# Attention of a decoder trunk: where TensorE takes its waits within a step

## The chip, the cores and the metric

The kernel runs on one core of a Trainium2 chip. The metric is the device time of one execution in microseconds (us). The engines are named as in the profile: PE is TensorE's matmuls, PEld its weight loads (they overlap the matmuls), DVE is VectorE, ACT is ScalarE, POOL is GpSimd, SP issues most DMAs. Each engine works through its own instructions in order, and engines wait for each other on semaphores.

## What is computed

A trunk of two layers on 1024 tokens of width 1024. Layer 0 mixes tokens by sparse attention with three branches (compressed blocks, selected blocks, a sliding window), layer 1 by attention to the 256 keys that an indexer selects. After each comes a gated convolutional feed-forward part; RMS norms stand around all of them. Cut to the part that the change touches:

```python
s_c = jnp.einsum('bqghd,bngd->bghqn', qb, k_cmp)      # compressed branch, "cmp"
s_s = jnp.einsum('bqghd,bgqkd->bghqk', qb, k_s)       # selected blocks, "full"
s_w = jnp.einsum('bqghd,bkgd->bghqk', qb, k_w)        # window, "near"
p = masked_softmax(s, mask)                           # for each branch
o = jnp.einsum('bghqk,bkgd->bqghd', p, v)
o = gb[..., 0:1] * o_c + gb[..., 1:2] * o_s + gb[..., 2:3] * o_w
```

## The kernel before, in words

The attention of a layer is a list of items, written out in full (no loop on the chip). There are 16 rounds, one for each pair of heads and each half of 512 tokens; in a round each branch takes its blocks of 128 keys in turn. An item is one key block for both heads of the pair, up to 512 queries wide (`cmp` is a single item). Layer 0 (`A0`, tiles `n_...`) has 208 items, layer 1 (`A1`, tiles `m_...`) 96. A planner (`AttentionPlan`) places all other work at the steps of this list by its own estimates of cost.

In step s TensorE does, in this order (`attention_pe`):

- the scores of item s+1 (`scores_pe`): for each of the two heads two products (L913, L915) and up to four small ones that add masks (L919). Each head's scores fill one of three PSUM banks in turn (a "unit", bank `u % 3`). Before each head it waits in `bank_free` until ScalarE's exponentials (L976, semaphore `a_ex`) have read the unit three before. For a `cmp` item there is one unit (L888 to L893).
- the ring (`ring_pe`): products that find the row maxima of a later round (`peak_pe`, L851 and, for `cmp`, L845) and one transpose of these maxima per round ("rows", L870). They share three other PSUM banks, `3 + y % 3`. Before ring entry y TensorE waits until VectorE (L1064/L1066, L1081, L1085, semaphore `a_md`) or, for rows, ScalarE (L999, `a_me`) has read entry y-3. A step has none to 13 entries, mostly one to four. The transpose waits besides for all maxima of its round (`a_md`, `a_mc`).
- the values of item s (`values_pe`, L931 and L937) into bank 6 or 7, after a wait for both exponentials of the item, and for the first item of a branch also for the eviction of the bank (L1008, `a_ov`);
- for some steps a branch's row sums (`divisors_pe`, L946 and L951), for which it waits for a bank and for GpSimd's sums (L992, `a_added`).

ScalarE's exponentials of an item run as soon as its scores are there, one head after the other. ScalarE also evicts a branch's result (L1008) into a tile that VectorE's product (L1120) must have freed, and that product needs the reciprocals of the row sums, which travel from ScalarE (L1014) over three DMAs (`n_R<-n_DR`, `r_save<-n_R`, `n_RB<-r_save`, L1178 to L1192). The queries of a round are loaded by DMA (L826) into one of three slots.

In the program a wait is carried by the instruction that follows it. If that one has more waits than it can carry, the further ones stand in an instruction of TensorE's queue of their own ahead of it.

Of the kernel before, what the change touches and what calls it, by code (L numbers as in the profile page):

```python
# [258 lines left out]
def trunk(nc, A, out):  # L259
    ctx = ExitStack()  # L260
    with ctx:
        def semaphore(name):
            return ctx.enter_context(nc.semaphore(name))
# [139 lines left out]
        def bank(b):  # L403
            return PS[:, b, :]
# [292 lines left out]
        def first_norm_pe(pe):  # L697
            for hf in range(2):
                for dt in range(DT):
# [6 lines left out]
        a_rot, a_t1, a_t2, a_qf, a_qhi, a_qlo, a_ready, a_pk, a_md, a_mc, a_me, a_ex, a_pv, a_ov = (  # L706
            semaphore("a_" + x) for x in ("rot", "t1", "t2", "qf", "qhi", "qlo", "ready", "pk", "md",
                                          "mc", "me", "ex", "pv", "ov"))
# [83 lines left out]
        def query_high(r, h, c0=0, w=HALF):  # L792
            return WH[:, r % 3, h * HALF + c0:h * HALF + c0 + w]

        def query_low(r, h, c0=0, w=HALF):
            return WL[:, r % 3, h * HALF + c0:h * HALF + c0 + w]

        def triangle(a):
            return a.B["MZ"][:, 4 * P:5 * P]

        def mask_tile(a, i, kb, count):
            first = i * (i + 1) // 2 + kb
            return a.B["MASK"][:, first:first + count, :].rearrange("p b n -> p (b n)")
# [34 lines left out]
        def peak_pe(pe, a, y, x):  # L838
            p = a.plan.peaks[x]
            if x == 0 or a.plan.peaks[x - 1].r != p.r:  # L840
                pe.wait_ge(a_slot[p.r % 3], a.queries_in(p.r))
            g = a.group(a.order[p.r][0])
            if p.kind == "cmp":
                for ii in range(4):
                    last = nc.tensor.matmul(PS[:, 3 + y % 3, ii * DH:(ii + 1) * DH],  # L845
                                            query_high(p.r, p.h, ii * P, P),
                                            a.B["KCA"][:, g, DH:2 * DH], start=True, stop=True)
            else:
                k0, w = peak_keys(a, p)
                KA = a.B[a.keys[p.kind][0]]  # L850
                last = nc.tensor.matmul(PS[:, 3 + y % 3, 0:w], query_high(p.r, p.h, p.ii * P, P),  # L851
                                        KA[:, g, k0:k0 + w], start=True, stop=True)
            last.then_inc(a_pk, 1)

        def ring_pe(pe, a, step):

            for y in a.plan.ring_at.get(step, ()):
                if y >= 3:
                    what, x = a.plan.ring[y - 3]
                    if what == "peak":  # L860
                        pe.wait_ge(a_md, a.md0 + x + 1)
                    else:
                        pe.wait_ge(a_me, a.me0 + x + 1)
                what, x = a.plan.ring[y]
                if what == "peak":
                    peak_pe(pe, a, y, x)
                else:
                    pe.wait_ge(a_md, a.md0 + a.plan.total[x])
                    pe.wait_ge(a_mc, a.mc0 + a.plan.extra[x])
                    nc.tensor.transpose(PS[:, 3 + y % 3, 0:P], a.B["NM"][:, x % 2, :],  # L870
                                        IDENT[:, :]).then_inc(a_pk, 1)

        def bank_free(pe, a, u):

            if u >= 3:
                pe.wait_ge(a_ex, a.qk0 + u - 2)

        def scores_pe(pe, a, s):
            n = a.plan.items[s]
            B, g, hf = a.B, a.group(a.order[n.r][0]), a.order[n.r][1]  # L880
            if s == a.plan.opens[n.r]:
                pe.wait_ge(a_slot[n.r % 3], a.rows_in(n.r))
            if n.kind == "cmp":
                u = n.u
                bank_free(pe, a, u)
                for h in range(2):
                    c = DH * (1 - h)
                    nc.tensor.matmul(bank(u % 3), B["KCA"][:, g, c:c + P], query_high(n.r, h),  # L888
                                     start=h == 0, stop=False)
                    nc.tensor.matmul(bank(u % 3), B["KCB"][:, g, c:c + P], query_low(n.r, h),  # L890
                                     start=False, stop=False)
                for ii in range(4):
                    last = nc.tensor.matmul(PS[:, u % 3, ii * P:(ii + 1) * P],  # L893
                                            B["CMPM"][:, 4 * hf + ii, :], B["IDB"][:, :],
                                            start=False, stop=ii == 3)
                last.then_inc(qk, 1)
                return
            KA, KB = (B[x] for x in a.keys[n.kind][0:2])
            keys = slice(n.kb * P, (n.kb + 1) * P)
            masks = []  # L900
            for ii in range(n.c0 // P, (n.c0 + n.w) // P):
                i = 4 * hf + ii
                if "MASK" in B and i >= 2:
                    masks.append((ii, mask_tile(a, i, n.kb, 1)))
                elif i == n.kb:
                    masks.append((ii, triangle(a)))
                elif n.far and i == n.kb + 4:
                    masks.append((ii, B["MZ"][:, 0:P]))
            for h in range(2):
                u = n.u + h  # L910
                bank_free(pe, a, u)
                dst = PS[:, u % 3, 0:n.w]
                nc.tensor.matmul(dst, KA[:, g, keys], query_high(n.r, h, n.c0, n.w),  # L913
                                 start=True, stop=False)
                last = nc.tensor.matmul(dst, KB[:, g, keys], query_low(n.r, h, n.c0, n.w),  # L915
                                        start=False, stop=not masks)
                for x, (ii, mask) in enumerate(masks):
                    o = ii * P - n.c0
                    last = nc.tensor.matmul(PS[:, u % 3, o:o + P], mask, B["IDB"][:, :],  # L919
                                            start=False, stop=x == len(masks) - 1)  # L920
                last.then_inc(qk, 1)

        def values_pe(pe, a, s):
            n = a.plan.items[s]
            B, g = a.B, a.group(a.order[n.r][0])
            b = 6 + n.rb % 2
            if n.first and n.rb >= 2:
                pe.wait_ge(a_ov, a.rb0 + n.rb - 1)
            if n.kind == "cmp":
                pe.wait_ge(a_ex, a.qk0 + n.u + 1)  # L930
                nc.tensor.matmul(bank(b), B["VC"][:, g, :], a.probabilities(n, 0), start=True,  # L931
                                 stop=True).then_inc(a_pv, 1)
                return
            pe.wait_ge(a_ex, a.qk0 + n.u + 2)
            V = B[a.keys[n.kind][2]]
            for h in range(2):
                last = nc.tensor.matmul(PS[64 * h:64 * h + 64, b, n.c0:n.c0 + n.w], V[:, g, n.kb, :],  # L937
                                        a.probabilities(n, h), start=n.first, stop=n.last)
            last.then_inc(a_pv, 1)
# [15 lines left out]
        def attention_pe(pe, a):  # L955
            pe.wait_ge(a_ready, a.ready0 + 5)
            plan = a.plan
            ring_pe(pe, a, -1)
            scores_pe(pe, a, 0)
            for s in range(plan.NI + 2):  # L960
                if s + 1 < plan.NI:
                    scores_pe(pe, a, s + 1)
                ring_pe(pe, a, s)
                if s < plan.NI:
                    values_pe(pe, a, s)
                for rb in plan.divisors_at.get(s, ()):
                    divisors_pe(pe, a, rb)
# [1776 lines left out]
```

## Time and profile before

| | |
|---|---|
| Median of 3 runs | 3386.02 us (3385.41 to 3388.66) |
| The profiled execution | 3384.83 us, its span 3383.0 us |
| Attention of layer 0 | about 296 to 885 us of the span |
| Attention of layer 1 | about 2173 to 2495 us |

A row of a timeline is: start in us, duration in us, engine, line, instruction, output and inputs, shapes, how many were merged into the row, and in brackets how long the engine had been idle before it and what ended the idle time ("issue": nothing that the profile shows). The idle time of PEld is not idle time of TensorE: matmuls may run in it. A row of waits gives who waited for whom, the total in us, how many times, and the longest. A chain of waits lists in order of time what each next piece was released by.
### The profile page before, as it was taken

The page shows a single profiled execution, that of the slowest core. Times are in us where ns is not written, and L with a number is a line of the kernel's source. Part 1 is how long each engine was busy: PE and PEld are TensorE (multiplying, and loading weights), DVE is VectorE, ACT ScalarE, POOL GpSimd, SP SyncE. Part 2 cuts the span into 40 slices and gives each one's busy share as a digit, 9 for nine tenths or more (in the row PEclk, how much of TensorE's full clock was granted, in tenths as well). Part 3 has the DMA queues.
Part 4 walks back from the last instruction along what each step waited for, and adds up shares of the span by engine and source line. Part 5 has one row for each costly group of instructions (what it writes and reads, how often), then busy time and mean ns, then how long its engine had stood idle before and what let it go on. Part 6 is the DMA issues. An engine that isn't in the chain of part 4 may idle for free.

```text
span 3383.0 us, 38562 instructions
## 1 busy us (share of the span) xinstructions
PE 2976.0 (88%) x13504; PEld 2177.6 (64%) x13504; DVE 2117.4 (63%) x3711; ACT 1453.6 (43%) x2519; POOL 701.9 (21%) x683
## 2 busy tenths in 40 slices
PE   7797989999879999999968664379997999999997
PEld 5684544445567888878856553244556788887885
DVE  6544455555366776677676699655436676667656
ACT  4342444444434544444433544333444454444443
POOL 2352454544300000000003035425630000000000
PEclk9787999999989999999989787689998999999999
DMA  5143221121322323333322022322132233333332
GB/s 166 44 110 91 48 45 43 39 52 39 116 69 88 97 90 100 99 93 96 94 87 77 0 56 81 94 63 58 42 104 75 87 94 94 100 94 94 98 110 73
DMA packets 360184, 270.51 MB, mean 80 GB/s; under 512 B 63941, under 2 KB 313863, under 8 KB 359479
## 3 DMA queue, kind: packets, MB, share of 16 engines
q1 hardware_dynamic: 358839, 265.96, 27.2%
q8 instruction: 107, 1.75, 0.2%
q10 hardware_dynamic: 1152, 2.10, 0.2%
q14 instruction: 86, 0.70, 0.1%
HBM read 233.46 MB, written 29.82 MB: 78 GB/s over the span
## 4 chain that ended last, share of the span: by engine, by line
PE 71%; DVE 10%; DMA 5%; issue 5%; ACT 4%; POOL 3%; SPq 2%; POOLq 0%; ACTq 0%; DVEq 0%
PE PS L510 18%; PE PS L512 17%; PE PS L511 17%; PE PS L937 5%; PE PS L913 3%; PE PS L851 3%; PE PS L915 2%; DMA n_RB<-r_save 1%; PE PS L919 1%; PE PS L951 1%; DMA WL<-ql_save 1%; DMA r_save<-n_R 1%; SPq L1999 1%; DVE RT_b L615 1%; DVE m_Z L2372 1%
## 5 line engine op out<-in xcount | busy, mean ns | idle before, releaser
L510 PE MATMUL PS<-HH,WH 128*128 128x512 f32 (+1 forms) x2160 | 860.0, 398 | 132.5 <-POOL WL L483 76.4
L511 PE MATMUL PS<-HL,WH 128*128 128x512 f32 (+1 forms) x2160 | 851.8, 394 | 0.0
L512 PE MATMUL PS<-HH,WL 128*128 128x512 f32 (+1 forms) x2160 | 850.5, 394 | 0.0
L510 PEld LDWEIGHTS PS<-HH,WH 128*128 128x128 f32 x2160 | 416.5, 193 | 228.3 <-issue 100.1
L511 PEld LDWEIGHTS PS<-HL,WH 128*128 128x128 f32 x2160 | 416.1, 193 | 87.5 <-issue 2.3
L512 PEld LDWEIGHTS PS<-HH,WL 128*128 128x128 f32 x2160 | 415.0, 192 | 86.7
L499 DVE TENSOR_TENSOR WL<-WR,WH 128x1024 fp32r<-128x1024 f32 x296 | 361.8, 1222 | 136.6 <-ACT WH L492 132.5
L492 ACT ACTIVATE WH<-WR 128x1024 fp32r<-128x1024 f32 x296 | 314.4, 1062 | 122.7 <-PE PS L512 89.9
L992 POOL TENSOR_TENSOR n_ACC<-n_ACC,n_PX 128x384 f32<-128x384 f32 (+3 forms) x320 | 286.2, 924 | 310.7 <-PE PS L937 187.2
L479 POOL TENSOR_TENSOR TOUCH<-WR 128x1 f32<-128x1 f32 x39 | 10.6, 271 | 1107.7 <-PE PS L512 1051.7
L1085 DVE CUSTOM_DVE_ANT_0 n_JUNK<-PS,n_MZ 128x512 bf16<-128x512 f32 (+2 forms) x320 | 146.1, 487 | 131.4 <-PE PS L851 130.0
L992 POOL TENSOR_TENSOR m_ACC<-m_ACC,m_PX 128x512 f32<-128x512 f32 (+3 forms) x160 | 157.8, 1012 | 172.7 <-PE PS L937 89.2
L976 ACT ACTIVATE n_PX<-PS 128x384 f32<-128x384 f32 (+3 forms) x320 | 134.1, 439 | 122.0 <-PE PS L919 103.5
L1431 DVE TENSOR_TENSOR Y_c<-PS,Y_c 128x512 f32<-128x512 f32 x160 | 107.0, 689 | 87.6 <-PE PS L512 87.2
L1431 DVE TENSOR_TENSOR Y_b<-PS,Y_b 128x512 f32<-128x512 f32 x160 | 107.0, 689 | 85.7 <-PE PS L512 85.3
L510 PE MATMUL PS<-HIDH_b,WH 128*128 128x512 f32 x352 | 141.7, 402 | 6.3 <-issue 3.2
L510 PE MATMUL PS<-HIDH_c,WH 128*128 128x512 f32 x352 | 141.9, 403 | 3.9 <-issue 3.2
L512 PE MATMUL PS<-HIDH_c,WL 128*128 128x512 f32 x352 | 139.3, 396 | 0.0
L512 PE MATMUL PS<-HIDH_b,WL 128*128 128x512 f32 x352 | 139.2, 396 | 0.0
L511 PE MATMUL PS<-HIDL_c,WH 128*128 128x512 f32 x352 | 139.1, 395 | 0.0
L511 PE MATMUL PS<-HIDL_b,WH 128*128 128x512 f32 x352 | 139.1, 395 | 0.0
L1085 DVE CUSTOM_DVE_ANT_0 m_JUNK<-PS,m_MASK 128x512 bf16<-128x512 f32 (+3 forms) x160 | 87.7, 594 | 55.6 <-PE PS L851 55.3
(384 smaller groups left out, 5264.5 us busy)
## 6 DMA issues: line engine op xcount, KB each, us to landing
WR<-in_ffn_w_up SPq DMA_DIRECT2D x176, 512.0 KB, 3.8
WR<-in_ffn_w_down SPq DMA_DIRECT2D x88, 512.0 KB, 3.6
WH<-qh_save SPq DMA_DIRECT2D x64, 256.0 KB
n_RB<-r_save SPq DMA_DIRECT2D x96, 128.0 KB, 3.1
WR<-in_nsa_w_out SPq DMA_DIRECT2D x16, 512.0 KB, 3.9
WL<-ql_save SPq DMA_DIRECT2D x32, 256.0 KB
WR<-in_dsa_w_in SPq DMA_DIRECT2D x16, 512.0 KB, 4.5
WR<-in_dsa_w_out SPq DMA_DIRECT2D x16, 512.0 KB, 4.1
```

The costliest lines, as they stand in the source:

```text
L492: nc.scalar.activation(WH[:, x, :], WR[:, r, :], ACT.Copy).then_inc(w_hi, 1)
L499: nc.vector.tensor_tensor(WL[:, x, :], WR[:, r, :], WH[:, x, :].bitcast(F32), ALU.subtract).then_inc(w_split, 1)
L510: nc.tensor.matmul(dst, wh, xh, start=start, stop=False)
L511: nc.tensor.matmul(dst, wh, xl, start=False, stop=False)
L512: return nc.tensor.matmul(dst, wl, xh, start=False, stop=stop)
L851: last = nc.tensor.matmul(PS[:, 3 + y % 3, 0:w], query_high(p.r, p.h, p.ii * P, P), KA[:, g, k0:k0 + w], start=True, stop=True)
L913: nc.tensor.matmul(dst, KA[:, g, keys], query_high(n.r, h, n.c0, n.w), start=True, stop=False)
L937: last = nc.tensor.matmul(PS[64 * h:64 * h + 64, b, n.c0:n.c0 + n.w], V[:, g, n.kb, :], a.probabilities(n, h), start=n.first, stop=n.last)
L976: nc.scalar.activation(a.probabilities(n, h), PS[:, (n.u + h) % 3, 0:n.w], ACT.Exp).then_inc(a_ex, 1)
L992: nc.gpsimd.tensor_tensor(total, total, a.probabilities(n, h), ALU.add).then_inc(a_added, 1)
L1085: nc.vector.tensor_tensor_reduce(out=B["JUNK"][:, x % 2, 0:w], in0=src, in1=mask, scale=1.0, scalar=-3e38, op0=ALU.add, op1=ALU.max, accum ...
L1431: nc.vector.tensor_tensor(y, bank(4 + x % 3), y, ALU.add).then_inc(f.da, 1)
```

## The change

Three waits of TensorE are placed elsewhere. Nothing else is changed: the same products in the same order, the same buffers, and no other engine's program.

1. Scores: the wait for the second head's bank is taken ahead of the first head's products, in place of the first one's own (it is for the later value of the same semaphore, and so covers it).
2. Ring: the waits for the first up to three entries of a step are all taken ahead of the first of them; a fourth and later entry keeps its wait in its place.
3. Values: their waits are taken ahead of the last ring entry of the step, or in their old place if the step has none.

The waits for a round's queries, for the rows in `scores_pe`, for the transpose and for the row sums stay where they were.

```diff
+        def ring_free(pe, a, y):
+            if y >= 3:
+                what, x = a.plan.ring[y - 3]
+                if what == "peak":
+                    pe.wait_ge(a_md, a.md0 + x + 1)
+                else:
+                    pe.wait_ge(a_me, a.me0 + x + 1)
+
         def ring_pe(pe, a, step):
-            for y in a.plan.ring_at.get(step, ()):
-                if y >= 3:
-                    what, x = a.plan.ring[y - 3]
-                    if what == "peak":
-                        pe.wait_ge(a_md, a.md0 + x + 1)
-                    else:
-                        pe.wait_ge(a_me, a.me0 + x + 1)
+            ys = a.plan.ring_at.get(step, ())
+            for y in ys[0:3]:
+                ring_free(pe, a, y)
+            for n, y in enumerate(ys):
+                if n >= 3:
+                    ring_free(pe, a, y)
                 what, x = a.plan.ring[y]
+                if y == ys[-1] and 0 <= step < a.plan.NI:
+                    values_ready(pe, a, step)
                 if what == "peak":
                     peak_pe(pe, a, y, x)
...
+            if not ys and 0 <= step < a.plan.NI:
+                values_ready(pe, a, step)
...
         def scores_pe(pe, a, s):
...
+            bank_free(pe, a, n.u + 1)
             for h in range(2):
                 u = n.u + h
-                bank_free(pe, a, u)
...
+        def values_ready(pe, a, s):
+            n = a.plan.items[s]
+            if n.first and n.rb >= 2:
+                pe.wait_ge(a_ov, a.rb0 + n.rb - 1)
+            pe.wait_ge(a_ex, a.qk0 + n.u + (1 if n.kind == "cmp" else 2))
+
         def values_pe(pe, a, s):
...
-            if n.first and n.rb >= 2:
-                pe.wait_ge(a_ov, a.rb0 + n.rb - 1)
             if n.kind == "cmp":
-                pe.wait_ge(a_ex, a.qk0 + n.u + 1)
...
-            pe.wait_ge(a_ex, a.qk0 + n.u + 2)
```

## Rows read from the trace of the kernel before

**Rows 1.** The page: span, busy time of the engines, chain by engine.

```profile
span 3383.0 us, 38562 instructions
...
PE 2976.0 (88%) x13504; PEld 2177.6 (64%) x13504; DVE 2117.4 (63%) x3711; ACT 1453.6 (43%) x2519; POOL 701.9 (21%) x683
...
PE 71%; DVE 10%; DMA 5%; issue 5%; ACT 4%; POOL 3%; SPq 2%; POOLq 0%; ACTq 0%; DVEq 0%
...
```

**Rows 2.** Windows of both attentions: stretch, engines' busy time, granted clock, DMA.

```profile
...
474.00:546.00 72.00, 65.72 (x339) 34.98 (x338) 39.91 (x121) 30.01 (x67) 35.85 (x40) 0.98 0.20 46
507.20:510.60 3.40, 3.40 (x10) 1.36 (x11) 1.18 (x5) 0.27 (x1) 0.65 (x1) 0.50 0.06 9
...
2400.00:2495.00 95.00, 92.52 (x566) 46.88 (x563) 40.47 (x114) 45.33 (x91) 64.68 (x62) 1.00 0.17 43
...
```

**Rows 3.** Waits of TensorE's matmuls in layer 0's attention, 296 to 885 us.

```profile
...
PE PS L913 <- ACT n_ACC L976: 13.8, 7, 2.8
PE PS L851 <- DVE n_NM L1085: 13.5, 17, 1.4
PE PS L870 <- DVE n_NM L1066: 10.1, 8, 1.5
PE PS L913 <- ACT n_PX L976: 8.2, 7, 1.2
...
```

**Rows 4.** Timeline of TensorE's weight loads, 449.4 to 452.1 us.

```profile
...
450.39 0.14 PEld L951 LDWEIGHTS PS<-n_ACC,ONES 128*64 128x64 f32 x2 [0.29 <-issue]
...
451.77 0.19 PEld L913 LDWEIGHTS PS<-WH,n_KWA 128*128 128x128 f32 x1 [0.81 <-issue]
...
```

**Rows 5.** Timeline of TensorE's matmuls in the same stretch.

```profile
...
450.82 1.03 PE L951 MATMUL PS<-n_ACC,ONES 128*64 128x512 f32 x4
451.78 0.38 PE L913 MATMUL PS<-WH,n_KWA 128*128 128x256 f32 x1
...
```

**Rows 6.** Timeline of the weight loads across a stall of layer 0.

```profile
...
487.43 0.19 PEld L913 LDWEIGHTS PS<-WH,n_KSA 128*128 128x128 f32 x1 [0.24 <-issue]
...
490.25 0.19 PEld L913 LDWEIGHTS PS<-WH,n_KSA 128*128 128x128 f32 x1 [2.21 <-ACT n_ACC L976]
...
490.59 0.69 PEld L851 LDWEIGHTS PS<-n_KSA,WH 128*128 128x128 f32 x3
...
```

**Rows 7.** Chain of waits that ends this stall.

```profile
...
485.25 3.06 DMA n_RB<-r_save
...
488.33 0.70 DVE n_TMP L1120
...
489.71 0.50 ACT n_ACC L976
...
```

**Rows 8.** Timeline of the weight loads after it, 494.9 to 497 us.

```profile
...
495.02 0.19 PEld L913 LDWEIGHTS PS<-WH,n_KSA 128*128 128x128 f32 x1 [2.09 <-ACT n_PX L976]
...
495.51 0.19 PEld L913 LDWEIGHTS PS<-WH,n_KSA 128*128 128x128 f32 x1 [0.19 <-ACT n_PX L976]
...
```

**Rows 9.** Timeline of the weight loads, 504.9 to 507.6 us.

```profile
...
505.05 0.54 PEld L845 LDWEIGHTS PS<-n_KCA,WH 128*128 128x128 f32 x4
507.11 0.14 PEld L870 LDWEIGHTS PS<-IDENT,n_NM 128*128 128x128 f32 x1 [1.52 <-DVE n_CS L1064]
...
```

**Rows 10.** Timeline of VectorE in the same stretch.

```profile
...
505.34 0.41 DVE L1064 TENSOR_TENSOR n_CS<-PS,n_CMPM 128x256 f32<-128x256 f32 x1
...
506.12 0.41 DVE L1064 TENSOR_TENSOR n_CS<-PS,n_CMPM 128x256 f32<-128x256 f32 x1
...
```

**Rows 11.** Timeline of the weight loads at the end of layer 0's attention.

```profile
...
874.51 0.19 PEld L913 LDWEIGHTS PS<-WH,n_KWA 128*128 128x128 f32 x1 [1.08 <-ACT n_PX L976]
...
```

**Rows 12.** Timeline of the weight loads, layer 1, first half.

```profile
...
2199.05 0.19 PEld L913 LDWEIGHTS PS<-WH,m_KDA 128*128 128x128 f32 x1 [0.17 <-issue]
...
2203.02 0.19 PEld L913 LDWEIGHTS PS<-WH,m_KDA 128*128 128x128 f32 x1 [3.35 <-ACT m_ACC L976]
...
```

**Rows 13.** Chain of waits, layer 1, 2262 to 2272 us.

```profile
...
2263.42 5.44 DMA WL<-ql_save
...
```

## Prediction

> **What bounds the kernel.** The page first: TensorE is busy for 88% of a span of 3383.0 us and carries 71% of the chain that ended last, VectorE 10% [rows 1]. The change touches only the two attentions, some 910 us of it (296 to 885 and 2173 to 2495 us). There the windows show TensorE busy for 65.7 of 72 us in layer 0 and for 92.5 of 95 us in the second half of layer 1, the next engine, VectorE or GpSimd, far behind [rows 2]. So TensorE's order and its stalls set the pace, and every wait put earlier in its queue counts in full unless it is over by then, or unless the time is given back in a later stall. The table of waits tells which are real: in layer 0 the matmuls stood idle 13.8 us for an exponential that starts a branch (7 times), 8.2 us for other exponentials (7), 13.5 us for VectorE's maxima (17), and 10.1 us for the transpose's last maxima (8) [rows 3]. Everything else is released before TensorE comes to it.
>
> **What a wait costs that is already over.** This decides whether fewer places with waits can pay. L951 carries one wait, and its second one stands in an instruction of its own ahead of it. Its weights are nevertheless loaded at 450.39 us, while the products before it run; its own matmul comes at 450.82 us [rows 4, 5]. So a wait that is over neither stops the early weight load nor shows a price, and nor does the extra instruction. I take 0 for each wait taken away and each one joined to another. Bounds: a gain of 0.10 us for each values product (second rival), and for the loss nothing that a row shows; I leave it inside the range. The Trainium skill has the rule ("TensorE: Matmul & The Clock Gate", "Step-by-step: what each phase is for"): weight loads are pulled ahead of running matmuls when row groups don't conflict or the background buffer is free. By it waits that are over don't enter; but it would also have the load of L913 pulled ahead behind L951, where the trace has it only at 451.77 us, with its matmul, so the row decides.
>
> **The parts.** An in-order engine on which waits only move forward gains nothing from them; what is left is to add up where they are not yet over.
>
> *Scores.* The second head's bank is free when the exponential of the item's predecessor, first head, is done. In most steps that is over before the first head's load: no cost. The places where it is not:
>
> - A. Seven stalls of layer 0 [rows 3]. One of them: the first head's load goes at 487.43 us, the second's only at 490.25 us [rows 6]. The first head's work sat in the shadow of a chain of DMA, VectorE's product and the exponential, which ends it whatever TensorE does [rows 7]. Now both heads come after it. From first load to second load is 0.49 us in a pair that runs without other hindrance [rows 8]. 7 x 0.49 = 3.4 us. Behind the stall wait the ring, the values, ScalarE's next exponentials and VectorE's maxima, and the chain goes on through them; nothing gives it back.
> - B. Some 5 us later in six rounds the first head starts at 495.02 us, straight after one exponential, and the second's bank is freed 0.45 us later (its load goes at 495.51 us) [rows 8]. TensorE loses 0.45 us, but here the chain runs beside it through DMAs until about 503 us, and TensorE then stands idle before the transpose: loads of L845 at 505.05, of the transpose only at 507.11 us [rows 9]. What comes out is worked out under the ring.
> - C. Seven places where the bank is free 0.10 us too late (382.79, 453.24 us and on): 0.7 us.
> - D. The end of layer 0: the pair at 872.87 us, whose second load waits until 874.51 us [rows 11], costs a first head of 384 columns, 0.46 us; two more (832.7 and 857.6 us) lie ahead of DMA chains and are taken at half, 0.4 us. Together 0.9 us.
> - E. Layer 1: the pair of 2199.05 us, with its second load at 2203.02 us after 3.35 us idle, and six like it until 2316 us [rows 12]. First heads there are 0.42 to 0.76 us long, 3.7 us together. Two of them (2264.5 and 2283.4 us) are followed by TensorE's wait for a load of queries, 5.44 us long in the first case, and hidden behind that [rows 13]: 2.9 us remain. In the second half of layer 1 none is late.
>
> *Ring.* Entries y+1 and y+2 must be free before y goes. In layer 1 they always are. In layer 0, 17 steps are late, by 7.3 us in all: four by 0.50 us right behind the stalls of A, where TensorE now comes 0.49 us later anyway (0 us); six by 0.28 us about 499 us and its like, where B has made TensorE late already (0 us); five by 0.49 to 0.78 us at the transpose, two by 0.03 us. The five: at 505.05 us the last L845 must now wait for the slot that VectorE's L1064 frees at 505.34 + 0.41 = 505.75 us, about 0.75 us later [rows 9, 10]. This takes up B's 0.45 us. Its four products, 0.61 us long, end about 506.45 us; VectorE took them at 506.12 us [rows 10], so the transpose and all behind it come about 0.35 us later. With B: 6 x 0.35 = 2.1 us.
>
> *Values.* Their exponentials are over at the last ring entry in every step of both layers, mostly by more than 1 us: 0 us. The cover is the ring and the scores between; where a step has no ring the wait stays.
>
> **Sum**: 3.4 + 2.1 + 0.7 + 0.9 + 2.9 = 10.0 us. The profiled execution took 3384.8 us, so 3394.8 us; it lies 1.2 us under the median of the runs, so the forecast is 3396.0 us, 0.3% slower. Without anything given back the local losses are 3.4 + 2.9 + 0.7 + 1.3 + 3.7 + 7.3 = 19.3 us; with A alone certain, 3.4 us. Some 0.2%, 6.8 us, is what can be told from no change.
>
> **The rivals.**
>
> - *Given back.* B, C, D and E lie in stretches with DMA chains; if only A comes through, and a part of E, the loss is 3.4 to 6 us: 3391 us, no difference. For it: 5.44 us waits for queries in layer 1 [rows 13]. Against: layer 0's chain runs through TensorE between the stalls. Chance 0.27.
> - *Faster: the values' weights are loaded early.* Place: the first load of L937 in the steps with a ring, about 250. It no longer carries a wait. If it was the wait, and not the change of tile from 128 to 64 columns, that kept it behind the last maxima product, it can now overlap it. Price: L951's products started 0.43 us apart with loads pulled ahead; L913 behind them comes 0.96 us after 450.82 us, where twice 0.43 would be 0.86 [rows 4, 5], so 0.10 us a time, 25 us: 3396 - 25 = 3371 us. It decides from 0.04 us a time (10 us). Against: L951 with its waits is pulled ahead. No row has a change of tile without a wait, so it stays open. Chance 0.08.
> - *Slower still: the clock.* The granted clock was 0.50 from 507.2 to 510.6 us, right behind an idle TensorE, 0.98 on average around it [rows 2]. Such a stretch costs at most half of its 3.4 us. Of the seven stalls of A only one was followed by it. The change makes their idle time unbroken, half a us longer; if the other six and four of E get one, 10 x 1.7 = 17 us more, 3413 us; with half of them 3405 us. The skill's page on TensorE ("Why this matters for your kernels") likewise says that idle gaps between bursts of matmuls cost the clock; by it this would be the likeliest case, by the one in seven of the trace it isn't. Chance 0.12.
> - The forecast itself: 0.53.
>
> **Numbers.** 3396.0 us. The range goes down to 3387 us, most of "given back", and up to 3406 us, all local losses or half of the clock's; outside are the faster rival and the end of the clock's. Slower by over 0.2%: 0.53 + 0.12 = 0.65, less a little for the forecast's lower edge and more for the rival's upper; 0.64. Within: 0.28. Faster: 0.08.
>
> **What would show it.** The count of late waits of L913 for ScalarE stays, but the first load of such a pair, no longer the second, carries it, at the same time in the stall, with both pairs behind it. The transposes' wait shrinks. The load of L937 still starts behind the last ring product: if it starts before it, the faster rival is right. Spans of the two attentions longer by 7 and 3 us, all other stages as before. A granted clock in layer 0 clearly under 0.98 means the clock. Wrong altogether if the attention is shorter.

## The result, and the profile after

The changed kernel takes 3397.9 us (median of 14 runs), the kernel before 3388.3 us (14 runs beside them): 9.6 us more. The ratio is 1.0026, 95% interval 1.0015 to 1.0037, so 5 to 12.5 us slower. The forecast was 10.0 us more, 3396.0 us. Single executions of either kernel lie 15 us apart and more (3383.8 to 3400.2 before), and the profiled one of the changed kernel, at 3393.5 us, is one of its faster ones. Three executions of 7251 to 11364 us (two of the kernel before, one of the last version below) are left out of the comparisons.

In the changed kernel lines have moved: L925 is L913 of before, L931 is L919, L947 L931, L952 L937, L966 L951, L880 L870, L991 L976, L1079 to L1100 are L1064 to L1085. The page, for [rows 1]:

```profile
span 3391.7 us, 38807 instructions
...
PE 2977.4 (88%) x13504; PEld 2180.6 (64%) x13504; DVE 2115.3 (62%) x3711; ACT 1454.8 (43%) x2519; POOL 702.7 (21%) x683
...
PE 72%; DVE 11%; DMA 5%; issue 5%; ACT 4%; POOL 3%; SPq 2%; POOLq 0%; ACTq 0%; DVEq 0%
```

The same work in the same busy time (2977.4 against 2976.0 us), with a span 8.7 us longer. By stages, with the windows of before first (the first stage is left out) and those of after behind them:

```profile
296.00:885.00 589.00, 537.63 (x2703) 285.49 (x2704) 310.86 (x960) 244.09 (x529) 286.21 (x320) 0.96 0.19 44
885.00:2173.00 1288.00, 1072.16 (x4534) 864.11 (x4534) 911.75 (x1374) 573.47 (x910) 145.63 (x113) 0.92 0.28 85
2173.00:2495.00 322.00, 287.51 (x1598) 148.28 (x1598) 157.06 (x466) 126.30 (x262) 157.76 (x160) 0.92 0.22 53
2495.00:3383.00 888.00, 838.61 (x3632) 680.65 (x3632) 582.06 (x739) 384.87 (x608) 0.00 (x0) 0.97 0.31 95
```

```profile
296.90:885.80 588.90, 532.58 (x2704) 284.34 (x2704) 308.73 (x960) 244.94 (x530) 287.13 (x320) 0.97 0.19 44
885.80:2173.00 1287.20, 1071.36 (x4533) 863.51 (x4533) 911.80 (x1374) 572.68 (x909) 145.67 (x113) 0.91 0.28 85
2173.00:2504.00 331.00, 293.50 (x1599) 151.87 (x1600) 158.29 (x467) 127.85 (x262) 157.72 (x160) 0.90 0.21 51
2504.00:3391.70 887.70, 839.06 (x3632) 681.01 (x3628) 581.06 (x739) 384.46 (x606) 0.00 (x0) 0.97 0.31 95
```

All else is as it was; layer 1's attention takes 331.0 us for 322.0, and layer 0's looks the same, where the forecast had 7 and 3 us more. That is a trap of the single profile: layer 0's granted clock is 0.97 for 0.96, layer 1's 0.90 for 0.92. How much of each layer ran at the low clock differs between executions, also where the code is the same. At a lower clock the same products keep TensorE busy for longer (layer 1: 293.5 us at 0.90, 287.5 at 0.92), so TensorE's idle time, the length of a window less its busy time, tells more than the length: in these rows it goes from 51.4 to 56.3 us in layer 0 and from 34.5 to 37.5 us in layer 1. The comparison below uses idle time, stretches without any low clock, and the medians of runs.

TensorE's waits in layer 0, for [rows 3]:

```profile
PE PS L925 <- ACT n_ACC L991: 18.4, 7, 3.5
...
PE PS L851 <- DVE n_NM L1100: 13.5, 17, 1.4
PE PS L925 <- ACT n_PX L991: 9.4, 9, 1.7
PE PS L880 <- DVE n_NM L1081: 8.5, 8, 1.1
```

The seven waits for a branch's first exponential went from 13.8 to 18.4 us, those for the others from 8.2 (7) to 9.4 (9), VectorE's maxima stayed at 13.5, the transpose's wait fell from 10.1 to 8.5. The stall of [rows 6], and the pair behind it of [rows 8]:

```profile
486.42 0.30 PEld L947 LDWEIGHTS PS<-n_ACC,n_VC 128*128 128x128 f32 x2
489.58 0.19 PEld L925 LDWEIGHTS PS<-WH,n_KSA 128*128 128x128 f32 x1 [2.87 <-ACT n_ACC L991]
...
489.92 0.19 PEld L925 LDWEIGHTS PS<-WH,n_KSA 128*128 128x128 f32 x1
...
490.49 0.44 PEld L851 LDWEIGHTS PS<-n_KSA,WH 128*128 128x128 f32 x3
```

```profile
495.31 0.19 PEld L925 LDWEIGHTS PS<-WH,n_KSA 128*128 128x128 f32 x1 [2.57 <-ACT n_PX L991]
...
495.65 0.19 PEld L925 LDWEIGHTS PS<-WH,n_KSA 128*128 128x128 f32 x1
```

Here is the mechanism in four rows. Before, the first head was loaded at 487.43 us and only the second waited. Now nothing of the pair goes before the end of the stall at 489.58 us, 2.87 us idle for the loader, and both heads and their low parts follow: the first maxima load comes 0.91 us after the end of the stall, where it came 0.34 us after it before (490.59 for 490.25) [rows 6]. That is 0.57 us more for this stall, of which the forecast had 0.49. At 495.31 us the second head's load no longer has a wait of its own and follows after 0.34 us.

### The profile page after: what moved, and what is told of

The parts are those of the page before. It is cut to its first block, busy times and chain, and to the rows that moved or that the text cites. A ratio compares the mean times of both kernels' runs of the same rounds, so it can differ in the third digit from the quotient of the medians.

```text
span 3391.7 us, 38807 instructions
## 1 busy us (share of the span) xinstructions
PE 2977.4 (88%) x13504; PEld 2180.6 (64%) x13504; DVE 2115.3 (62%) x3711; ACT 1454.8 (43%) x2519; POOL 702.7 (21%) x683
## 4 chain that ended last, share of the span: by engine, by line
PE 72%; DVE 11%; DMA 5%; issue 5%; ACT 4%; POOL 3%; SPq 2%; POOLq 0%; ACTq 0%; DVEq 0%
PE PS L510 18%; PE PS L511 17%; PE PS L512 17%; PE PS L952 5%; PE PS L925 4%; PE PS L851 3%; PE PS L927 2%; PE PS L931 1%; PE PS L966 1%; DMA n_RB<-r_save 1%; DMA WL<-ql_save 1%; SPq L2014 1%; DVE m_Z L2387 1%; DVE RT_b L615 1%; PE PS L664 1%
## 5 line engine op out<-in xcount | busy, mean ns | idle before, releaser
L510 PE MATMUL PS<-HH,WH 128*128 128x512 f32 (+1 forms) x2160 | 860.6, 398 | 132.5 <-POOL WL L483 77.8
L510 PEld LDWEIGHTS PS<-HH,WH 128*128 128x128 f32 x2160 | 416.6, 193 | 228.5 <-issue 98.1
L1100 DVE CUSTOM_DVE_ANT_0 n_JUNK<-PS,n_MZ 128x512 bf16<-128x512 f32 (+2 forms) x320 | 146.1, 487 | 139.2 <-PE PS L851 138.2
L991 ACT ACTIVATE n_PX<-PS 128x384 f32<-128x384 f32 (+3 forms) x320 | 134.0, 437 | 120.7 <-PE PS L931 116.4
L510 PE MATMUL PS<-HIDH_b,WH 128*128 128x512 f32 x352 | 142.3, 404 | 6.3 <-issue 3.2
L510 PE MATMUL PS<-HIDH_c,WH 128*128 128x512 f32 x352 | 141.9, 403 | 3.9 <-issue 3.2
L1100 DVE CUSTOM_DVE_ANT_0 m_JUNK<-PS,m_MASK 128x512 bf16<-128x512 f32 (+3 forms) x160 | 87.7, 594 | 61.1 <-PE PS L851 60.7
```

The costliest lines, as they stand in the source:

```text
L510: nc.tensor.matmul(dst, wh, xh, start=start, stop=False)
L991: nc.scalar.activation(a.probabilities(n, h), PS[:, (n.u + h) % 3, 0:n.w], ACT.Exp).then_inc(a_ex, 1)
L1100: nc.vector.tensor_tensor_reduce(out=B["JUNK"][:, x % 2, 0:w], in0=src, in1=mask, scale=1.0, scalar=-3e38, op0=ALU.add, op1=ALU.max, accum ...
```

## The experiments

Each ran beside the kernel before on the same chip. The first eight are the kernel before with one part of the change or a piece of one, or with waits added. The last four move work of ScalarE and VectorE; one of them starts from the changed kernel.

### The three parts alone

**Scores alone** (part 1):

```diff
+            bank_free(pe, a, n.u + 1)
             for h in range(2):
                 u = n.u + h
-                bank_free(pe, a, u)
```

> Part 1 of the change alone: the second head's bank is waited for ahead of the first head's scores; ring and values as before. Theory (waits count only where they are not yet over, and this part has nearly all such places): TensorE's first scores start at the end of each of the seven stalls of layer 0, and the loss of the change is nearly all there: 7 to 10 us over the kernel before, of it 3 us or more in layer 1. Rival 'extra instructions' (the 245 wait instructions that the change adds to TensorE's queue cost about 40 ns each): this part adds none, so 0 us. Rival 'ring' (the loss is in the gathered maxima waits): 0 to 2 us.

Measured: 3395.5 us against 3385.9, ratio 1.0027 (1.0017 to 1.0037), 9.6 us slower (5.8 to 12.5). By the medians this is the whole loss.

**Ring alone** (part 2, `ring_free` for `ys[0:3]` ahead of the loop):

> Part 2 alone: the waits of a step's first three ring entries ahead of the first. Theory: without part 1 nothing has made TensorE late, so its own late places show: 0.50 us at four stalls, and little at the transposes, 2 to 4 us in layer 0, 0 in layer 1. Rival 'extra instructions': 161 added wait instructions at 40 ns, 6 us, spread evenly over both layers. Rival 'ring': 8 us or more.

Measured: 3386.3 us, ratio 1.0002 (0.9990 to 1.0014): no difference. The 2 to 4 us expected in layer 0 don't show; the interval reaches to 4.7 us, so they aren't excluded either, and its one clean stretch of layer 0 (below) is a long one.

**Values alone** (part 3, `values_ready` ahead of the last ring entry):

> Part 3 alone: the values' waits ahead of the last ring entry. Theory: 0 us; the exponentials are over by then, and the first weight load behind the last maxima product starts as late as before (320 to 370 ns after the start of a 512 column product), since the change of tile holds it, not the wait. Rival 'early load': 10 to 25 us faster. Rival 'extra instructions': 186 of them at 40 ns, 7 us slower.

Measured: 3387.4 us, ratio 1.0004 (0.9992 to 1.0016): no difference, and 10 us faster is excluded. Whether the load can start early is seen in the changed kernel, at a place of the same shapes in both. The weight loads before, where L937 carries a wait that is long over, and after, where L952 carries none:

```profile
452.48 0.20 PEld L851 LDWEIGHTS PS<-n_KSA,WH 128*128 128x128 f32 x1
452.87 0.20 PEld L937 LDWEIGHTS PS<-n_PX,n_VW 128*64 128x64 f32 x4 [0.19 <-issue]
```

```profile
451.91 0.20 PEld L851 LDWEIGHTS PS<-n_KSA,WH 128*128 128x128 f32 x1
452.30 0.20 PEld L952 LDWEIGHTS PS<-n_PX,n_VW 128*64 128x64 f32 x4 [0.19 <-issue]
```

Both start 0.39 us after the load of the maxima product. It is the same at the other places of layer 0 at full clock: behind a maxima product of 512 columns the first values load starts 0.37 us (median) after the start of that product in the kernel before (60 places), in this one (60) and in the changed one (63). So it isn't the wait that holds the load back. What is left is the change of tile, from 128 to 64 columns; no run varies that alone.

### Waits that are over

```diff
                 bank_free(pe, a, u)
+                pe.wait_ge(proj, a.q0 + 2 * PAIRS)
+                pe.wait_ge(a_ready, a.ready0 + 5)
...
+                    pe.wait_ge(a_ready, a.ready0 + 5)
                 what, x = a.plan.ring[y]
...
             pe.wait_ge(a_ex, a.qk0 + n.u + 2)
+            pe.wait_ge(a_ready, a.ready0 + 5)
```

> The kernel before with waits added that are always over, two ahead of each head's scores and one ahead of each ring entry and each values product; 1424 more wait instructions in TensorE's queue than before. Theory: a wait that is over costs nothing, 0 to 3 us, unless so many in a row keep the queue from running ahead. Rival 'extra instructions': 1424 x 40 ns = 57 us slower.

Measured: 3388.9 us against 3385.9, ratio 1.0005 (0.9994 to 1.0016). At the upper end 5.4 us for 1424 wait instructions, under 4 ns each. At that price the 245 that the change adds are worth less than 1 us; the rival of extra instructions is out.

### Layer by layer

The condition `a.n == 0` or `a.n == 1` around part 1, so that it holds in one layer:

> Part 1 in layer 0 only. Theory by the profiles so far: layer 0's attention gets 4 to 5 us longer for the same low-clock time (the seven stalls at 0.49 us and the chains behind them), layer 1's stays at 322 to 326 us; total 4 to 5 us slower. Rival 'clock': layer 0 not longer once low-clock time is taken off at half, total 0 to 2 us.

> Part 1 in layer 1 only. Rival 'clock': TensorE's idle stretches in layer 1's first half are no longer broken by a first head's scores, some 10 us more of it run at the low clock, and layer 1's attention takes 331 us against 322 to 326; total 5 to 7 us slower, and nothing left once low-clock time is taken off at half. My forecast's term (local losses only): 3 us, with low-clock time as before.

Measured: layer 0 alone 3393.5 us against 3386.9, ratio 1.0019 (1.0008 to 1.0031), 6.7 us; layer 1 alone 3389.8 us, ratio 1.0011 (0.9998 to 1.0023), 3.0 us (-0.7 to 7.8), which taken alone is not clear of none. The forecast had 3.4 + 2.1 + 0.7 + 0.9 = 7.1 us and 2.9 us. My later expectation, that layer 1 would lose 5 to 7 us by the clock, was read off one profile; the median doesn't bear it out, and the interval doesn't exclude it.

What the clock does in layer 1 stays partly open. Three stretches of it, before and with part 1 in layer 1 (two of its irregular first half, one of its second):

```profile
2231.13:2279.12 47.99, 38.54 (x195) 19.66 (x193) 29.90 (x75) 16.79 (x39) 16.20 (x19) 0.86 0.29 67
2279.12:2324.08 44.96, 39.11 (x209) 19.59 (x207) 19.79 (x67) 15.62 (x34) 16.59 (x19) 0.92 0.30 72
2357.69:2395.30 37.61, 37.00 (x220) 18.85 (x218) 20.02 (x63) 16.64 (x31) 22.20 (x22) 1.00 0.23 55
```

```profile
2229.54:2280.85 51.31, 40.47 (x194) 20.97 (x192) 29.95 (x75) 17.20 (x39) 16.36 (x19) 0.80 0.25 63
2280.85:2327.44 46.59, 40.45 (x208) 20.74 (x206) 19.87 (x67) 16.11 (x34) 16.42 (x19) 0.89 0.28 69
2361.06:2398.68 37.62, 37.02 (x220) 18.86 (x218) 20.05 (x63) 16.66 (x31) 22.25 (x22) 1.00 0.22 55
```

The second half is the same to 0.01 us, as forecast. The first half is longer by 3.3 and 1.6 us, at a granted clock of 0.80 and 0.89 for 0.86 and 0.92; 1.9 and 1.3 us of that is TensorE's busy time for the same products. But an unchanged layer 1 can have that as well; this is its whole attention in the run below in which only layer 0 was edited:

```profile
2167.10:2499.50 332.40, 298.53 (x1600) 153.85 (x1600) 156.50 (x467) 127.09 (x262) 157.11 (x160) 0.88 0.22 51
```

332.4 us at 0.88, longer than the changed kernel's 331.0. Over the seven profiles with an unchanged layer 1 it took 322 to 332 us, over the three with part 1 in it 330 to 333. TensorE's idle time parts them better. Taken from the attention's first product to the next stage's first load, it is 32.9 to 36.2 us in the seven (mean 34.6) and 37.3 to 38.2 us in the three (mean 37.7), so 3.1 us more, close to the forecast's 2.9. Whether part 1 also brings more low clock here stays open: those windows have 0.88 to 0.92 in the seven and 0.89 to 0.90 in the three.

### The seven stalls against the other places of layer 0

Part 1 only at the second item of each round of layer 0 (the diff), or only elsewhere in layer 0 (the condition turned round behind `a.n == 0`):

```diff
+            if a.n == 0 and s and a.plan.items[s - 1].first and n.kind == 'full':
+                bank_free(pe, a, n.u + 1)
             for h in range(2):
                 u = n.u + h
-                bank_free(pe, a, u)
+                if not (a.n == 0 and s and a.plan.items[s - 1].first and n.kind == 'full'):
+                    bank_free(pe, a, u)
```

> Part 1 only at the 16 places in layer 0 where a round's second item starts, which holds the seven stalls (term A), and nowhere else. Between the starts of two rounds 71 us apart, in stretches with no low clock, the kernel before takes 70.1 to 70.6 us and part 1 everywhere in layer 0 71.3 to 71.4. By the forecast's terms A is 0.49 us of that: 70.6 to 71.1 us here, 3 to 4 us slower in all. Rival 'A is nothing, the rest is all': 70.1 to 70.6 us. Rival 'all is A': 71.3 us.

> Part 1 in layer 0 everywhere but at those 16 places (terms B, C and D). By the forecast's terms the transposes' chain and the places 0.10 us late give 0.35 + 0.10 us in a clean stretch of 71 us, so 70.5 to 71.0 us, and about 1 us at the end of layer 0: 3 to 4 us slower in all. Rival 'B is given back in the transposes' wait': 70.1 to 70.6 us, only the end longer, 1 us in all. Rival 'they only count together': here and in the other run nothing.

Measured in time: 3393.0 us against 3388.6, ratio 1.0019 (1.0007 to 1.0032), and 3392.6 us, ratio 1.0011 (0.9995 to 1.0027): 4.5 and 4.0 us, the second not clear of none (-1.7 to 9.1), and too near for the times to part them. The clean stretches do it better. Each runs from the first scores of a round to those of the round two further on, at a granted clock of 1.00. In this order: before, the changed kernel, stall places only, other places only.

```profile
607.76:678.30 70.54, 64.33 (x340) 34.54 (x338) 38.90 (x123) 30.27 (x67) 35.86 (x40) 1.00 0.21 47
```

```profile
607.26:678.33 71.07, 64.23 (x341) 34.43 (x339) 38.66 (x123) 30.28 (x67) 35.83 (x40) 1.00 0.20 46
```

```profile
606.77:677.92 71.15, 64.27 (x340) 34.48 (x339) 38.96 (x123) 30.25 (x67) 35.89 (x40) 1.00 0.20 46
```

```profile
462.25:532.90 70.65, 64.38 (x340) 34.61 (x339) 38.96 (x123) 30.14 (x67) 35.84 (x40) 1.00 0.21 47
```

Ten profiles have 28 such stretches. Ten in kernels without parts 1 and 2 in layer 0 take 70.10 to 71.71 us, median 70.5. Nine with part 1 in all of layer 0: 71.03 to 71.55, median 71.1. Stall places only: 70.52, 71.08, 71.15. Other places only: 70.61, 70.64, 70.65, 70.72 and 71.97. The ring alone has a single one, 71.27. So part 1 costs about 0.65 us in 71. By the medians the stall places alone give 0.6 and the others alone 0.2, but with three and five stretches, which spread by 0.6 and 1.4 us, these two are rough.

There are six such stretches in layer 0, with six of the seven stalls: 3.9 us. The last two rounds, with the seventh stall and the places of term D, are longer. They run from their first scores to the first load of the next stage (L510); of the kernels so far five are clean there. The changed kernel's row and the ring alone's:

```profile
821.76:887.17 65.41, 58.69 (x301) 29.13 (x300) 22.28 (x54) 35.28 (x73) 36.82 (x40) 1.00 0.18 46
```

```profile
823.77:887.03 63.26, 58.72 (x301) 29.26 (x299) 23.37 (x54) 35.16 (x73) 37.74 (x40) 1.00 0.19 47
```

The other clean ones are 65.35 us (scores alone), 65.03 (other places only) and 63.34 (values alone): 2.1 us more with all of part 1, 1.7 with the other places only. Together that is 6.0 us, beside 6.7 by the times. Idle time says the same. From the first product of the attention to L510's first load TensorE idles 48.1 to 51.9 us in the five profiles without part 1 in layer 0 (mean 50.2) and 54.9 to 57.4 in the three with it (mean 56.4), 6.2 us more; 53.3 with the stall places only, 54.0 with the others only.

### What the stalls are, and a version that is faster

ScalarE stands in the eviction of a branch (L1008) until VectorE's product has read the tile, with the next exponential queued behind it. The eviction one step later:

```diff
-                if s < plan.NI and plan.items[s].last:
-                    evict_act(act, a, plan.items[s].rb)
+                if 1 <= s <= plan.NI and plan.items[s - 1].last:
+                    evict_act(act, a, plan.items[s - 1].rb)
```

> The kernel before, with ScalarE's eviction of a branch (L1008) one step later, behind the next item's exponentials. It tests what the stalls of A are: if ScalarE waits in the eviction for VectorE's product and holds the next exponential up behind it, the seven waits of L913 for the exponential of n_ACC (13.8 us) shrink to under 5 us, and the kernel gets 5 to 12 us faster. If the DMA chain sets the end of the round anyway, the wait only moves (to the bank of the values, a_ov) and the time stays within 2 us.

> The changed kernel with the same later eviction. If the loss of part 1 in layer 0 is its late places behind ScalarE's stalled eviction, most of it is gone with them: at most 1 to 2 us slower in layer 0 than e7, in layer 1 as much as in e6 unless its stalls go too. If the loss is something else, it stays at 4 to 5 us over e7 in layer 0.

Measured: 3390.4 us against 3386.9 for the first, ratio 1.0012 (0.9996 to 1.0027), no gain; 3391.1 us, ratio 1.0009 (0.9997 to 1.0021) for the change with it. With the stall of ScalarE gone, the change costs 0.7 us by the medians instead of 9.6. That fits the theory but doesn't show it: with both intervals anything up to some 7 us is possible. And the wait only moved, not to the bank of the values, as the expectation's second case had it, but to VectorE. TensorE's waits in layer 0 of the first of the two, then VectorE beside such a place:

```profile
PE PS L851 <- DVE n_NM L1085: 23.7, 32, 1.9
...
PE PS L870 <- DVE n_NM L1066: 12.2, 8, 2.7
...
PE PS L913 <- ACT n_PX L976: 2.1, 6, 0.5
```

```profile
491.38 0.69 DVE L1120 TENSOR_TENSOR n_TMP<-n_OP,n_RB 128x512 f32<-128x512 f32 x1 [2.51 <-DMA n_RB<-r_save]
...
492.72 0.55 DVE L1085 CUSTOM_DVE_ANT_0 n_JUNK<-PS,n_MZ 128x384 bf16<-128x384 f32 x1
```

The waits for exponentials fell from 22.0 to 2.1 us, those for maxima rose from 13.5 to 23.7: VectorE now stands idle for 2.51 us ahead of the product that needs the DMA chain, with the maxima queued behind it. So that product too has to go later in its engine's program:

```diff
-            self.apply_at.setdefault(self.step(t + 11.5), []).append(rb)
+            self.apply_at.setdefault(self.step(t + 13.5), []).append(rb)
-                self.low_at.setdefault(self.step(t + 13.5), []).append(rb // self.nb)
+                self.low_at.setdefault(self.step(t + 15.5), []).append(rb // self.nb)
```

The eviction moves as above, by one step (`items[s - 1]`) or by two (`items[s - 2]`).

> The kernel before with ScalarE's eviction one step later, as in the earlier run, and VectorE's product that waits for the DMA chain (L1120) about 2 us later in its program, behind more maxima. In the earlier run the stall had only gone over to VectorE, which stood 2.5 us ahead of that product with maxima queued behind. If that was all, the waits of L913 for the exponential and of L851 for VectorE's maxima (13.8 and 12.8 us in layer 0 before) both fall, together to under 12 us, and the kernel gets 5 to 12 us faster. If the freed bank or tile is then late instead, they stay at 20 us or more and the time within 3 us.

> The same with the eviction two steps later: should ScalarE in the run with one step again stand in the eviction because the product comes later, this one is freer. Expected 0 to 4 us faster than that run; if the values' first product of a branch then waits for its bank, up to 5 us slower than it, with waits of L937 for L1008 in the table.

Measured: 3379.6 us against 3388.6, ratio 0.9977 (0.9965 to 0.9989), with the eviction one step later; 3377.3 us, ratio 0.9968 (0.9956 to 0.9980), with two: 11 us faster than the kernel before and 20 us under the changed one. The waits of layer 0 in the latter, and both attentions' windows:

```profile
PE PS L870 <- DVE n_NM L1066: 10.7, 8, 1.5
PE PS L851 <- DVE n_NM L1085: 8.5, 16, 1.8
...
PE PS L937 <- ACT n_OP L1008: 1.7, 2, 1.4
PE PS L913 <- ACT n_PX L976: 1.5, 1, 1.5
```

```profile
297.40:860.30 562.90, 534.26 (x2704) 287.68 (x2704) 319.11 (x960) 244.16 (x529) 284.36 (x320) 0.96 0.20 45
2146.50:2488.40 341.90, 301.86 (x1598) 154.69 (x1600) 157.75 (x466) 125.69 (x261) 156.62 (x160) 0.87 0.21 49
```

Waits for exponentials and maxima together came from 35.5 to 10.0 us, and layer 0's attention from 589 to 563 us. Layer 1, whose second half had no such stall, takes 342 us for 322, at a granted clock of 0.87 for 0.92; an unchanged layer 1 reached 332, so the price is some 10 to 20 us and its cause wasn't looked into. The edit in layer 0 alone is the obvious next version; it was not run.

## Why the prediction was right

- **What bounds.** TensorE's own order did, and its late waits were the ones named. Stages outside the attentions kept their times.
- **Waits that are over cost nothing.** Shown directly, at under 4 ns each. With it stands the step built on it, that waits which only move forward gain an in-order engine nothing: no part gained. The Trainium skill's rule ("TensorE: Matmul & The Clock Gate", "Step-by-step: what each phase is for"), by which the load is pulled ahead when row groups don't conflict or the load goes to the background weight buffer, fits the load of L951 at 450.39 us [rows 4]. The first values load behind a maxima product, at 0.37 us with a wait or without, doesn't follow from it as it stands.
- **Term A**, 3.4 us: 0.49 us for each of seven stalls. The clean stretches give 0.6, the stall shown above 0.57. It is half or more of what layer 0 loses. The 0.49 us was right in size by luck: it was read from the pair of 495.02 us [rows 8], whose second load itself waited 0.19 us for an exponential and which term B counts as hindered. An unhindered pair, as at 495.31 us in the changed kernel, has 0.34 us from load to load; the cost is the first head's two products of 512 columns ahead of the second's.
- **Terms B and C and the ring**, 2.8 us: 0.45 us in a stretch by the forecast, 0.2 measured in six, about 1.3 us in all, as far as five stretches tell. This term was sized too large. It said that the last L845 is held until VectorE frees its slot and that the transpose then comes 0.35 us late. In the changed kernel nothing holds it at that place: its load follows the mask's at once, and the transpose's row and VectorE's are

```profile
505.30 0.54 PEld L845 LDWEIGHTS PS<-n_KCA,WH 128*128 128x128 f32 x4
506.99 0.14 PEld L880 LDWEIGHTS PS<-IDENT,n_NM 128*128 128x128 f32 x1 [1.15 <-DVE n_CS L1079]
```

```profile
505.99 0.42 DVE L1079 TENSOR_TENSOR n_CS<-PS,n_CMPM 128x256 f32<-128x256 f32 x1 [1.16 <-PE PS L845]
```

VectorE had come to rest and waited 1.16 us for TensorE; before it had still been busy with older maxima when L845 was loaded [rows 9, 10]. From that load to the transpose's it is 1.69 us now and was 2.06. This one pair doesn't make it the work of the change: the kernel before has both lengths itself, 2.05 to 2.08 us at four of its six such places and 1.68 at two. One of these:

```profile
721.11 0.54 PEld L845 LDWEIGHTS PS<-n_KCA,WH 128*128 128x128 f32 x4
722.79 0.14 PEld L870 LDWEIGHTS PS<-IDENT,n_NM 128*128 128x128 f32 x1 [1.15 <-DVE n_CS L1064]
```

It goes by when VectorE is done with the product that waits for the DMA chain (L1120), which ended 0.24 us ahead of the load of L845 in the kernel before (503.16 + 1.65 = 504.81 us) and 1.87 us ahead of it in the changed one (502.48 + 0.95 = 503.43 us). Over the four profiles with an unchanged layer 0 in which the ring waits are unchanged too (before, values alone, extra waits, scores in layer 1) the short length comes at 12 of 24 places, over the three with part 1 in all of layer 0 at 16 of 18. So TensorE's delay is taken back in the transpose's wait where VectorE was still behind, and that is at about half the places; the forecast had it taken back only in part, and VectorE behind at all six. The hold on L845 does exist: at the first place of this kind, at 362 us, its load waits 0.46 us in the changed kernel, and with the ring alone it waits about 0.5 us at three of seven places.
- **Term D**, 0.9 us: 1.7 measured, in the last two rounds with the other places only. This term was sized too small. It took two of its three places at half because DMA chains follow them; that discount shows nowhere: the first of them (832.7 us) alone costs 0.6 us (from the first scores of its round to those of the next 22.56 us for 21.95). That B, C and the ring are 1.5 us too large and D 0.8 us too small partly cancels in the sum.
- **Term E**, 2.9 us: 3.0 by the medians, 3.1 by TensorE's idle time, with the part of the clock open.
- **Ring and values**, 0 us behind part 1: no difference alone either, within 5 us.

Of the rivals, "given back" has a piece in the transposes, not the whole. The faster one is out: no load starts earlier without its wait. The clock one has no sign in layer 0: the three profiles with part 1 in it have a granted clock of 0.95 to 0.97 there, the five without it 0.95 to 0.96. In layer 1 it isn't settled. That the sum of 10.0 us meets 9.6 so closely is partly luck: the interval is 5 to 12.5 us, and two of the terms were off in opposite directions.

## What to carry to other kernels

In an in-order engine a wait that is already over is nearly free (under 4 ns here), wherever it stands, and gathering such waits buys nothing; a wait that is not over yet should stand as late as possible, since each instruction in front of it runs in the shadow of the stall. To end a stall, follow it through all engines that queue behind it: here ScalarE's eviction and VectorE's product had to move together, and one alone only handed the wait on.

## What had not been expected of the hardware

1424 more wait instructions in TensorE's queue changed the time by 0.05% (-0.06 to 0.16%). And one and the same code of layer 1 takes 322 to 332 us, at a mean granted clock of 0.92 to 0.88, most of it in TensorE's busy time (289 to 299 us), little in its idle time (33 to 36 us); a difference of under 10 us in this stage's length between two single profiles says little, unless clock and idle time are read beside it.
